# Forty modulation tiles moved from TensorE blocks in the first mixer to VectorE row products in three up projections

## The chip, the cores and the metric

One core of one Trainium2 chip runs the whole program. The metric is the device time of one execution in microseconds (us). The times are medians over runs of the same program. TensorE is called PE here, VectorE DVE, ScalarE ACT, GpSimd POOL and the engine that issues weight loads SP.

## The reference, cut to what matters

The reference is a stack of float32 layers on 256 tokens of width 1024, with 256 context tokens in its second half. First comes a block of an RWKV and a Hyena mixer, a convolutional feed-forward network, an embedding, attention, a second such network and embedding. Then follow two layers that are modulated by a condition:

```python
s_lat = jax.nn.silu(c)[:, None, :]
s_ctx = jax.nn.silu(c_ctx)
for l in range(DEPTH):                                   # DEPTH = 2
    ml = jnp.split(s_lat @ w_mod[l] + b_mod[l], 9, axis=-1)   # w_mod[l]: 1024 x 9216
    mc = jnp.split(s_ctx @ w_mod[l] + b_mod[l], 9, axis=-1)
    x = half_ffn(x, g_norm[l, 0], ml[0], ml[1], ml[2], ...)
    ...  # token mixing with ml[3:6], a second half_ffn with ml[6:9]
```

The two products with `w_mod` give 2 x 9216 numbers for each of the two conditions, that is 144 tiles of 128 numbers, kept in `sb_mod` as `mod[128, 144, 2]`. Each must be there before the layer that uses it: tiles 0 to 71 are layer 0 (its first half feed-forward uses 0 to 23), tiles 72 to 95 the first half feed-forward of layer 1, the rest what follows.

## The kernel before, in words

Activations lie with features on the 128 partitions. Weights stream through a ring of four buffers of 2 MB, loaded on SP's queue; a buffer is loaded again when the last matmul of its block is done.

The 144 tiles come from two mechanisms.

- **Row products on DVE.** A tile of 128 rows of the transposed `w_mod` (512 KB) is loaded on ACT's queue by `scalar_rows_load`, into one of three buffers in the convolutional feed-forward networks (44 tiles), and into one of two buffers in the half feed-forward networks. `vector_row(R, t, s)` multiplies it with the silu of condition s and sums along the row: one scalar_tensor_tensor of 128x1024, so two per tile. The load of tile t waits until both products of tile t - 2 are done.
- **Blocks on PE.** Ten blocks of four tiles (`MOD_BY_PE`) are computed in the RWKV and Hyena mixer. A block is a 2 MB load on SP, two pieces of eight matmuls of 32 output rows by 256 columns, a copy on ACT (L966), two narrow column matmuls that turn the row, and an addition on DVE (L975). `Fill` steps the four generators `tensor_modulation`, `scalar_modulation` and `vector_modulation` at fixed places: `to(n)` runs the generator up to step n. Pieces stand in `tensor_hyena`, after most steps of `tensor_lora`, ahead of the recurrence, one in each of the four scans, and a last pair of column matmuls behind them.

The order of each engine is written out by hand, and semaphores alone tie them together. In the mixer the path is: Hyena (transposes, 32 spectral matmuls, inverse), gate matmuls, eight low-rank steps n (two matmuls, then two Sigmoids on ACT, L623 and L624, double buffered), `scalar_prepare` and `vector_prepare` (the last instruction of the operands is L784), and the scans.

The three half feed-forward networks with 512 tokens (half00, half01, half10) each run `Fast`: an up projection of 22 iterations i = 0 to 21, each with seven products of Strassen's scheme in the order 1, 5, 6, 7, 3, 2, 4, then a down projection of four double iterations. In one iteration:

- PE's product 4 waits for `st_v` (L1706 on DVE), product 7 of the next iteration for `st_c21` (L1741), product 1 of the next for a Silu on ACT (L1636).
- DVE's order is: weight sum 0 of the next iteration (L1661), L1699, weight sums 1 and 2, L1706, L1708, L1710, L1713, weight sum 3, **middle rows**, L1741, two products into the hidden tile (L1750, L1753), **late rows**. Before, iterations 1 to 19 have one middle and one late row product. Iteration 20 has two middle ones, the addition of the bias (L1502), and then the first two weight sums of the down projection (128x1408) ahead of L1741.
- ACT loads row tile i in iteration i, right behind its copy of product 1 (L1629).
- SP's next 2 MB of weights are issued at the end of product 4 of odd iterations.

Of the kernel before, what the change touches and what calls it, by code (L numbers as in the profile page):

```python
# [40 lines left out]
ROWS_EACH, ROWS_CONV = 20, FT  # L41
MOD_BY_PE = [(0, 16), (0, 17)] + [(1, b) for b in (0, 1, 2, 3, 4, 5, 16, 17)]
# [57 lines left out]
def build(nc, ins, out):  # L100
# [346 lines left out]
    def tensor_idle(n):  # L447

        for _ in range(n):
            mm(aux[3][:, 0:128], ones[:], ones[:])  # L450
# [58 lines left out]
    def tensor_hyena(other):  # L509
        other.to(2)  # L510
# [6 lines left out]
        other.to(3)  # L517
# [10 lines left out]
        for ft in range(2):  # L528
            te.wait_ge(hy_prod.sem, hy_prod_at(ft))
            for ct in range(4):  # L530
                if ft == 0:
                    te.wait_ge(hy_spec.sem, hy_spec_at(4 + ct))
                for part in range(2):
                    ins_ = mm(aux[ct][:, 0:L], yri[:, part, ft, 128 * ct:128 * ct + 128], dft[:, 2 + part, ft, :],
                              ft + part == 0, ft + part == 2)
                if ft:
                    hy_inv.on(ins_)
            if ft == 0:
                other.to(4)
        other.to(5)  # L540

    def vector_hyena(other):
# [17 lines left out]
        other.to(4)  # L560
# [7 lines left out]
        other.to(5)  # L568

    def scalar_hyena(other):  # L570
        other.to(2)
        ac.wait_ge(hy_t.sem, hy_t_at(0))
        hy_tm.on(ac.copy(s_tm[:, 0, :], aux[0][:]))
        other.to(3)
# [7 lines left out]
        other.to(5)  # L582
# [31 lines left out]
    def scalar_lora(other, first):  # L614
# [5 lines left out]
        for n in range(NG):  # L620
# [4 lines left out]
            if 1 <= n < 7:  # L625
                other.to(5 + n)
# [3 lines left out]
    def tensor_lora(other, first):  # L630
# [8 lines left out]
        for n in range(NG):  # L639
# [7 lines left out]
            if 1 <= n < 7:  # L647
                other.to(5 + n)
# [13 lines left out]
    sil, pick = area(work, 12416, KT, 32), area(work, 12672, 2, 2)  # L662
# [16 lines left out]
    sil_set, pick_set = signal("condition_silu_set"), signal("partial_picker_set")  # L679
    sil_at, pick_at = sil_set.reserve(1), pick_set.reserve(1)  # L680
# [64 lines left out]
    def vector_prepare():  # L745
# [17 lines left out]
        yield  # L763
        shifted_mix(r_, 0)
        shifted_mix(v_, 16)
        yield
# [7 lines left out]
        yield  # L774
# [10 lines left out]
        yield  # L785
# [4 lines left out]
        yield  # L790
# [128 lines left out]

    mod_blocks = [(l, b, block(1, banks=(2, 3))) for l, b in MOD_BY_PE]  # L920
    n_mod = len(mod_blocks)
    mod_row, mod_cols = signal("modulation_row_copied"), signal("modulation_columns")
    mod_row_at, mod_cols_at = mod_row.reserve(n_mod), mod_cols.reserve(n_mod)
    mod_rows = (rs_buf, rope[:, 3, :])

    def sync_modulation():
        for l, b, blk in mod_blocks:
            wv = ins["w_mod_2"][l].rearrange("(k p) n -> p k n", p=128)
            sync_load(blk, [(slots[blk.slot][:, :].rearrange("p (k n) -> p k n", k=KT), wv[:, :, b * 512:b * 512 + 512])])

    def tensor_modulation():
        def columns(j):
            g, row = mod_blocks[j][2].groups[0], mod_rows[j % 2]
            te.wait_ge(mod_row.sem, mod_row_at(j))
            for c in range(2):
                ins_ = mm(acc[g.bank][:, 4 * c:4 * c + 4], row[:, 128 * c:128 * c + 128], area(work, 12672, 4))
            mod_cols.on(ins_)

        te.wait_ge(sil_set.sem, sil_at(0))
        te.wait_ge(pick_set.sem, pick_at(0))  # L940
        for j, (l, b, blk) in enumerate(mod_blocks):
            g = blk.groups[0]
            te.wait_ge(weights_in[blk.slot].sem, blk.arrived_at)
            if g.free_at:
                te.wait_ge(acc_free[g.bank].sem, g.free_at)
            w = slots[blk.slot][:, :].rearrange("p (k n) -> p k n", k=KT)
            for q in range(8):
                k, t = 2 * (q // 4) + q % 2, q % 4
                mm(acc[g.bank][32 * t:32 * t + 32, 0:256], sil[:, k, :], w[:, k, 256 * (t // 2):256 * (t // 2) + 256], q < 4, False)
            yield  # L950
            if j:
                columns(j - 1)
            for q in range(8):
                k, t = 4 + 2 * (q // 4) + q % 2, q % 4
                ins_ = mm(acc[g.bank][32 * t:32 * t + 32, 0:256], sil[:, k, :], w[:, k, 256 * (t // 2):256 * (t // 2) + 256], False, q >= 4)
            acc_full.on(ins_)
            yield
        columns(n_mod - 1)
        yield

    def scalar_modulation():
        for j, (l, b, blk) in enumerate(mod_blocks):
            g = blk.groups[0]
            yield
            ac.wait_ge(acc_full.sem, g.done_at)
            mod_row.on(ac.copy(mod_rows[j % 2][:, 0:256], acc[g.bank][:, 0:256]))  # L966
            yield
        yield

    def vector_modulation():  # L970
        def add(j):
            l, b, blk = mod_blocks[j]
            g, at = blk.groups[0], 72 * l + 4 * b
            ve.wait_ge(mod_cols.sem, mod_cols_at(j))
            acc_free[g.bank].on(ve.tensor_tensor(  # L975
                mod[:, at:at + 4, :].rearrange("p (n c) s -> p c n s", n=2), acc[g.bank][:, 0:8].rearrange("p (c n s) -> p c n s", c=2, n=2),
                cols("b_mod", 4, at).rearrange("p (n c) -> p c n", n=2).unsqueeze(3).to_broadcast([128, 2, 2, 2]), ALU.add))

        for j in range(n_mod):
            yield  # L980
            if j:
                add(j - 1)
            yield
        add(n_mod - 1)
        yield

    class Fill:


        def __init__(self, steps):  # L990
            self.steps, self.taken = steps, 0

        def to(self, count):
            while self.taken < count:
                self.taken += 1
                next(self.steps, None)

    MOD_STEPS, MOD_EARLY, MOD_FIRST = n_mod * 2 + 1, 11, 16  # L1000

    def scan_fill(p):
        return MOD_FIRST + (p + 1) * (MOD_STEPS - 1 - MOD_FIRST) // NP

# [27 lines left out]
    def tensor_scan(p, other, ahead):  # L1032
# [34 lines left out]
        other.to(scan_fill(p))  # L1067
# [102 lines left out]
    def scalar_scan(p, other, ahead):  # L1170
# [5 lines left out]
        for lv in range(1, 6):  # L1176
# [31 lines left out]
            if lv == 2:  # L1208
                a_step.on(ac.copy(dd, dd_next))
            elif lv == 3:  # L1210
                next(ahead, None)
                sc_kept.on(ac.copy(rho, kr[:, :, 1, :]))
            elif lv == 4:
                next(ahead, None)
            elif lv == 1:
                other.to(scan_fill(p))
# [6 lines left out]
    def vector_scan(p, other, ahead):  # L1223
# [11 lines left out]
        for lv in range(1, 6):  # L1235
# [22 lines left out]
            if lv == 1:  # L1258
                other.to(scan_fill(p))
# [27 lines left out]
    def tensor_recurrence(other, first):  # L1287
        for _ in first:
            pass
        other.to(MOD_FIRST)  # L1290
        for p in range(NP):
            tensor_scan(p, other, tensor_ahead(p + 1) if p + 1 < NP else iter(()))
        tensor_scan_out(NP - 1)
        other.to(MOD_STEPS)

    def scalar_recurrence(other, first):
# [3 lines left out]
        other.to(MOD_FIRST)  # L1300
        for p in range(NP):
            scalar_scan(p, other, scalar_ahead(p + 1) if p + 1 < NP else iter(()))
        scalar_scan_out(NP - 1)
        other.to(MOD_STEPS)

    def vector_recurrence(other):
        vector_scan_setup()
        for n, _ in enumerate(vector_prepare()):
            if n in (1, 2, 3):
                other.to((MOD_EARLY, MOD_FIRST - 2, MOD_FIRST)[n - 1])  # L1310
        for p in range(NP):
            vector_scan(p, other, vector_ahead(p + 1) if p + 1 < NP else iter(()))
        vector_scan_out(NP - 1)
        other.to(MOD_STEPS)

    def gpsimd_rope():
        gp.wait_ge(sc_out.sem, sc_out_at(NP - 1))
        g = mod_blocks[-1][2].groups[0]
        gp.wait_ge(acc_free[g.bank].sem, g.freed_at)
# [142 lines left out]
    class ModRows:  # L1462
        def __init__(self, first, n=ROWS_EACH, cond=row_cond, tiles=row_tile, junk=row_junk):
# [5 lines left out]
            self.done = rows_done.reserve(2 * n)  # L1469

# [149 lines left out]
    def scalar_fast(F, following=None):  # L1620
        u, v, g1, g2 = F.temps
        for i in range(F.start, F.n):
# [7 lines left out]
            if F.rows and 2 <= i < ROWS_EACH:  # L1630
                scalar_rows_load(F.rows, i)
# [41 lines left out]
    def vector_fast(F, gate_of=None, following=None):  # L1673
# [8 lines left out]
        for i in range(F.start, F.n):  # L1682
# [35 lines left out]
            if F.rows and 1 <= i <= ROWS_EACH:  # L1718
                vector_row(F.rows, i - 1, 0)
                if i == ROWS_EACH:  # L1720
                    vector_row(F.rows, i - 1, 1)
# [25 lines left out]
            else:  # L1747
# [6 lines left out]
                if F.rows and 1 <= i < ROWS_EACH:  # L1754
                    vector_row(F.rows, i - 1, 1)
# [836 lines left out]
    half00 = HalfFfn(0, 0, 0, ple1.x_ready, extra=(ctx_in, 32), squares=area(big, FT * L, KT, T2), rows=ModRows(2 * ROWS_CONV))  # L2592
    mix0 = Mixing(0, True, half00.x_ready, hooked=True)
    half01 = HalfFfn(0, 1, 0, mix0.x_ready, squares=area(big, 0, KT, T2), rows=ModRows(72 + 24))
    half10 = HalfFfn(1, 0, 0, half01.x_ready, squares=hook_sq, hooked=True, rows=ModRows(72 + 24 + ROWS_EACH))
# [3 lines left out]
    def sync_program():  # L2599
# [10 lines left out]
        sync_modulation()  # L2610
# [31 lines left out]
    def tensor_program():  # L2642
# [3 lines left out]
        fill = Fill(tensor_modulation())  # L2646
        tensor_hyena(fill)
        first = tensor_prepare()
        tensor_lora(fill, first)
        tensor_recurrence(fill, first)  # L2650
# [228 lines left out]
```

## Time and profile before

| | |
|---|---|
| Runs | 3010.04, 3012.65, 3015.83 us; median 3012.65 |
| Profiled execution | 3011.66 us |
| its span | 3010.4 us |
| PE busy | 2894.4 us, 96% |
| DVE busy | 1609.2 us, 53% |
| ACT busy | 614.1 us, 20% |
| mean granted PE clock | 0.993 of 2.4 GHz |

The span goes from the first to the last instruction; the execution is 1.3 us longer. The mixer with the PE blocks ends at 312 us. The three up projections lie at about 1070 to 1338, 1786 to 2050 and 2194 to 2461 us.

### The profile page before, as it was taken

The page shows a single profiled execution, that of the slowest core. Times are in us where ns is not written, and L with a number is a line of the kernel's source. Part 1 is how long each engine was busy: PE and PEld are TensorE (multiplying, and loading weights), DVE is VectorE, ACT ScalarE, POOL GpSimd, SP SyncE. Part 2 cuts the span into 40 slices and gives each one's busy share as a digit, 9 for nine tenths or more (in the row PEclk, how much of TensorE's full clock was granted, in tenths as well). Part 3 has the DMA queues.
Part 4 walks back from the last instruction along what each step waited for, and adds up shares of the span by engine and source line. Part 5 has one row for each costly group of instructions (what it writes and reads, how often), then busy time and mean ns, then how long its engine had stood idle before and what let it go on. Part 6 is the DMA issues. An engine that isn't in the chain of part 4 may idle for free.

```text
span 3010.4 us, 41500 instructions
## 1 busy us (share of the span) xinstructions
PE 2894.4 (96%) x17066; PEld 2364.9 (79%) x17066; DVE 1609.2 (53%) x3259; ACT 614.1 (20%) x1388; POOL 37.5 (1%) x60
## 2 busy tenths in 40 slices
PE   8988999998999999999998999999999999999999
PEld 7767788984888978888643458888878888765999
DVE  4367467435466466673314546665366663225675
ACT  1245221134221121000214520000020000224110
POOL 0000000020000000000000000000000000000000
PEclk9999999999999999999999999999999999999999
DMA  6551465662565633322303013432344323331444
GB/s 237 187 198 32 141 214 158 197 182 84 177 214 147 192 131 129 117 79 77 112 26 112 29 56 126 137 117 58 110 146 131 120 72 81 110 108 55 142 142 111
DMA packets 344496, 376.17 MB, mean 125 GB/s; under 512 B 8723, under 2 KB 283556, under 8 KB 343540
## 3 DMA queue, kind: packets, MB, share of 16 engines
q1 hardware_dynamic: 324788, 306.65, 32.8%
q10 hardware_dynamic: 17312, 61.55, 5.6%
q0 software_dynamic: 2208, 5.31, 0.9%
q8 instruction: 137, 2.24, 0.3%
q14 instruction: 51, 0.42, 0.0%
HBM read 372.44 MB, written 1.05 MB: 124 GB/s over the span
## 4 chain that ended last, share of the span: by engine, by line
PE 90%; DVE 5%; ACT 4%; issue 1%; DMA 0%; ACTq 0%; DVEq 0%
PE acc L135 75%; PE aux L135 14%; ACT sb_xn L283 1%; PE aux L2433 1%; ACT L272 0%; DVE sb_work L2159 0%; DVE sb_work L2156 0%; ACT sb_work L1958 0%; ACT sb_work L1960 0%; DVE sb_xn L259 0%; DVE sb_work L1661 0%; PE acc L1045 0%; ACT sb_rstd L274 0%; DVE sb_work L1938 0%; DVE sb_work L2170 0%
## 5 line engine op out<-in xcount | busy, mean ns | idle before, releaser
L135 PE MATMUL acc<-sb_xn,weights 128*128 128x256 f32 (+2 forms) x5184 | 1217.7, 390 | 22.3 <-DVE sb_xn L259 14.0
L135 PEld LDWEIGHTS acc<-sb_xn,weights 128*128 128x128 f32 x5184 | 946.7, 191 | 247.5 <-issue 125.2
L135 PE MATMUL acc<-sb_work 128*128 128x256 f32 (+1 forms) x1944 | 375.0, 346 | 0.0
L135 PEld LDWEIGHTS acc<-sb_work 128*128 128x128 f32 x1944 | 324.4, 191 | 34.7 <-issue 0.4
L135 PE MATMUL acc<-sb_work,weights 128*128 128x256 f32 (+2 forms) x1508 | 322.4, 361 | 3.2 <-DVE sb_work L1394 1.4
L135 PE MATMUL acc<-sb_big,weights 128*128 128x256 f32 (+1 forms) x1776 | 313.8, 333 | 3.9 <-DVE sb_work L1815 3.8
L135 PEld LDWEIGHTS acc<-sb_big,weights 128*128 128x128 f32 x1776 | 278.1, 191 | 30.6 <-issue 5.2
L135 PEld LDWEIGHTS acc<-sb_work,weights 128*128 128x128 f32 x1508 | 254.2, 191 | 50.5 <-issue 21.8
L1629 ACT COPY sb_work<-acc 128x256 f32<-128x256 f32 (+1 forms) x112 | 38.0, 339 | 690.2 <-PE acc L135 690.2
L1699 DVE TENSOR_TENSOR sb_work<-sb_work,acc 128x256 f32<-128x256 f32 (+1 forms) x112 | 42.6, 381 | 228.8 <-PE acc L135 228.8
L135 PE MATMUL aux<-sb_xn,sb_work 128*128 128x256 f32 (+1 forms) x704 | 152.2, 360 | 8.4 <-ACT sb_xn L283 8.4
L1634 ACT ACTIVATE sb_work<-sb_work 128x256 f32<-128x256 f32 (+1 forms) x88 | 34.4, 391 | 572.4 <-DVE sb_work L1713 572.4
L1661 DVE TENSOR_TENSOR sb_work<-weights 128x512 f32<-128x512 f32 (+1 forms) x112 | 99.7, 890 | 95.5 <-PE acc L135 95.1
L135 PEld LDWEIGHTS aux<-sb_xn,sb_work 128*128 128x128 f32 x704 | 123.7, 194 | 24.3 <-issue 10.0
L135 PE MATMUL aux<-sb_big,sb_work 128*128 128x128 f32 (+3 forms) x592 | 109.3, 339 | 0.0
L1741 DVE TENSOR_TENSOR sb_work<-sb_work,acc 128x256 f32<-128x256 f32 (+1 forms) x112 | 42.5, 379 | 116.0 <-PE acc L135 115.9
L1661 DVE TENSOR_TENSOR weights<-weights 128x512 f32<-128x512 f32 (+1 forms) x112 | 99.6, 890 | 3.0
L1661 DVE TENSOR_TENSOR sb_work<-sb_work,weights 128x512 f32<-128x512 f32 (+1 forms) x112 | 99.2, 886 | 2.8 <-issue 0.2
L1661 DVE TENSOR_TENSOR sb_work<-weights,sb_work 128x512 f32<-128x512 f32 (+1 forms) x112 | 99.1, 884 | 0.7
L1713 DVE TENSOR_TENSOR sb_work<-sb_work,aux 128x256 f32<-128x256 f32 (+1 forms) x112 | 42.4, 378 | 104.2 <-PE aux L135 104.2
L135 PEld LDWEIGHTS aux<-sb_big,sb_work 128*128 128x128 f32 (+1 forms) x592 | 88.7, 185 | 10.9 <-issue 2.8
L135 PE MATMUL acc<-sb_xn,sb_work 128*128 128x128 f32 (+1 forms) x528 | 91.8, 331 | 4.2 <-DVE sb_xn L1666 4.2
(353 smaller groups left out, 2716.0 us busy)
## 6 DMA issues: line engine op xcount, KB each, us to landing
weights<-ffn_w_up SPq DMA_DIRECT2D x88, 1024.0 KB, 9.1
weights<-ffn_w_down SPq DMA_DIRECT2D x48, 1408.0 KB, 7.2
weights<-ffn_w_gate SPq DMA_DIRECT2D x44, 1024.0 KB, 5.4
sb_work<-w_mod_rows ACTq DMA_DIRECT2D x60, 512.0 KB, 6.2
sb_big<-w_mod_rows ACTq DMA_DIRECT2D x44, 512.0 KB, 4.8
weights<-w_mod SPq DMA_DIRECT2D x10, 2048.0 KB, 8.1
weights<-w_in SPq DMA_DIRECT2D x8, 2048.0 KB, 8.7
weights<-mix_w_in SPq DMA_DIRECT2D x6, 2048.0 KB, 12.5
```

Of the source, the lines that this page charges most:

```text
L135: return te.matmul(o, lhsT, rhs, start=start, stop=stop, skip_group_check=True)
L283: shifted.on(ac.activation(y, y, ACT.Identity, bias=N.shift(k, h)))
L1629: st_u.on(ac.copy(u[:, s, :], bank_a[:, 0:F.H]))
L1634: st_g2.on(ac.activation(g2[:, s, :], g2[:, s, :], ACT.Silu))
L1661: st_s.on(ve.tensor_tensor(to, one, other, op))
L1699: st_b.on(ve.tensor_tensor(u, u, bank_b[:, 0:F.H], ALU.add))
L1713: st_c12.on(ve.tensor_tensor(g2, g2, bank_e[:, 0:F.H], ALU.add))
L1741: st_c21.on(ve.tensor_tensor(u, u, bank_c[:, 0:F.H], ALU.add))
L2433: ins_ = te.transpose(aux[u % 3][:, c:c + 128], mx_e[:, u % 4, W * i + 128 * kt:W * i + 128 * kt + 128], ident[:])
```

## The change

```diff
-ROWS_EACH, ROWS_CONV = 20, FT
-MOD_BY_PE = [(0, 16), (0, 17)] + [(1, b) for b in (0, 1, 2, 3, 4, 5, 16, 17)]
+ROWS_HALF, ROWS_UNTIL, ROWS_CONV = (34, 33, 33), 20, FT
...
+            self.upto = lambda i: 2 * n * i // ROWS_UNTIL
...
-            if F.rows and 2 <= i < ROWS_EACH:
-                scalar_rows_load(F.rows, i)
+            if F.rows and 2 <= i <= ROWS_UNTIL:
+                for t in range(F.rows.upto(i - 2) // 2 + 2, min(F.rows.upto(i - 1) // 2 + 2, F.rows.n)):
+                    scalar_rows_load(F.rows, t)
...
-            if F.rows and 1 <= i <= ROWS_EACH:
-                vector_row(F.rows, i - 1, 0)
-                if i == ROWS_EACH:
-                    vector_row(F.rows, i - 1, 1)
+            if F.rows and 1 <= i <= ROWS_UNTIL:
+                middle = (F.rows.upto(i - 1) + F.rows.upto(i) + 1) // 2 if i < ROWS_UNTIL else F.rows.upto(i)
+                for n in range(F.rows.upto(i - 1), middle):
+                    vector_row(F.rows, n // 2, n % 2)
+                if i == ROWS_UNTIL:
                     vector_rows_bias(F.rows)
...
-                if F.rows and 1 <= i < ROWS_EACH:
-                    vector_row(F.rows, i - 1, 1)
+                if F.rows and 1 <= i < ROWS_UNTIL:
+                    for n in range(middle, F.rows.upto(i)):
+                        vector_row(F.rows, n // 2, n % 2)
```

Beside this, `sync_modulation`, `tensor_modulation`, `scalar_modulation`, `vector_modulation`, `Fill` and every `other.to(...)` are deleted, with the first Silu of the condition on ACT (L2670) and two small instructions on DVE (L2695, L2697) that served the blocks. half00 takes tiles 44 to 77, half01 78 to 110, half10 111 to 143. The number of row buffers (two) and their size stay.

## Rows read from the trace of the kernel before

**Rows 1.** The page's chain that ended last, shares of the span by engine.
```profile
PE 90%; DVE 5%; ACT 4%; issue 1%; DMA 0%; ACTq 0%; DVEq 0%
```

**Rows 2.** Timeline from 118 us: start, duration, engine, line, operation, count [idle before].
```profile
124.03 1.07 PE L135 MATMUL acc<-weights,sb_work 128*32 128x256 f32 x16
...
142.75 1.07 PE L135 MATMUL acc<-weights,sb_work 128*32 128x256 f32 x16
...
151.08 0.47 ACT L623 ACTIVATE sb_work<-aux,sb_cols 128x256 f32<-128x256 f32 x1
...
157.94 1.67 PE L135 MATMUL acc<-weights,sb_work 128*32 128x256 f32 x16 [4.30 <-DVE sb_mod L975]
```

**Rows 3.** Timeline from 160 us, the end of the preparation of the first scan.
```profile
172.31 1.28 ACT L1297 ACT_TABLE_LOAD   x1
...
175.83 0.63 ACT L805 ACTIVATE sb_work<-sb_work 128x512 f32<-128x512 f32 x1
...
177.50 0.68 DVE L776 TENSOR_TENSOR sb_work<-sb_work 128x512 f32<-128x512 f32 x1
...
180.75 0.69 DVE L784 TENSOR_TENSOR sb_work<-sb_work 128x512 f32<-128x512 f32 x1
```

**Rows 4.** Busy time of PE, PEld, DVE, ACT, POOL by stretch; PEclk, DMA share, GB/s.
```profile
159.00:165.00 6.00, 6.00 (x40) 2.74 (x36) 0.17 (x1) 2.19 (x5) 0.00 (x0) 0.50 0.25 77
...
171.00:177.00 6.00, 3.97 (x44) 2.08 (x43) 0.97 (x3) 5.20 (x9) 0.00 (x0) 1.00 1.04 375
```

**Rows 5.** Timeline from 211 us, the second scan, and from 308 us.
```profile
217.99 0.65 DVE L1231 TENSOR_TENSOR sb_xn<-sb_big 128x512 f32<-128x512 f32 x1
...
218.75 1.15 PE L135 MATMUL aux<-sb_big,sb_xn 64*64 64x64 f32 x32 [0.17 <-issue]
...
312.48 0.61 PE L135 MATMUL acc<-sb_work,sb_rope 128*128 128x4 f32 x4
```

**Rows 6.** Timeline of ACT from 0 and from 570 us: the first Sin, a table load.
```profile
24.97 0.42 ACT L440 ACTIVATE sb_work<-sb_work 64x256 f32<-64x256 f32 x1 [10.66 <-DVE sb_work L415]
...
588.23 1.28 ACT L1869 ACT_TABLE_LOAD   x1
592.61 0.38 ACT L1869 ACTIVATE sb_work<-acc 128x256 f32<-128x256 f32 x1 [3.09 <-PE acc L135]
```

**Rows 7.** Timeline from 1150 us, one iteration of half00's up projection (an odd one).
```profile
1159.19 0.34 ACTq L1476 DMA_DIRECT2D sb_work<-w_mod_rows  x1
...
1160.44 0.69 DVE L1661 TENSOR_TENSOR sb_work<-weights 128x512 f32<-128x512 f32 x1 [1.29 <-PE acc L135]
...
1163.90 0.42 DVE L1706 TENSOR_TENSOR sb_work<-sb_work,acc 128x256 f32<-128x256 f32 x1
...
1167.08 1.89 PE L135 MATMUL acc<-sb_work,weights 128*128 128x256 f32 x8
...
1171.27 0.33 ACTq L1476 DMA_DIRECT2D sb_work<-w_mod_rows  x1
```

**Rows 8.** Row loads: KB each, us to landing, in windows 1159:1161, 2294:2296, 1267:1269.
```profile
sb_work<-w_mod_rows ACTq DMA_DIRECT2D x1, 512.0 KB, 3.5
...
sb_work<-w_mod_rows ACTq DMA_DIRECT2D x1, 512.0 KB, 6.4
...
sb_work<-w_mod_rows ACTq DMA_DIRECT2D x1, 512.0 KB, 7.4
```

**Rows 9.** A wait of PE in the timeline, and the stretch behind it as in rows 4.
```profile
718.17 1.12 PE L2082 MATMUL aux<-sb_ident,sb_work 128*128 128x128 f32 x4 [3.18 <-DVE sb_work L2170]
...
718.00:720.00 2.00, 1.83 (x8) 1.42 (x10) 1.90 (x7) 0.79 (x4) 0.00 (x0) 0.51 1.10 360
```

**Rows 10.** Timeline from 1300 us, iterations 20 and 21 of half00's up projection.
```profile
1324.95 1.23 DVE L1496 SCALAR_TENSOR_TENSOR sb_work<-sb_work 128x1024 f32<-128x1024 f32 x1
...
1329.85 0.41 DVE L1741 TENSOR_TENSOR sb_work<-sb_work,acc 128x256 f32<-128x256 f32 x1
...
1331.11 1.89 PE L135 MATMUL acc<-sb_xn,weights 128*128 128x256 f32 x8
```

More of the change, by code:

```diff
@@ L445, in scalar_filter, with tensor_idle @@
             filt_rn.on(ac.activation(f_rn, f_rn, ACT.Exp, scale=-0.5))
-    def tensor_idle(n):
+    def tensor_idle(n, bank=aux[3]):
         for _ in range(n):
-            mm(aux[3][:, 0:128], ones[:], ones[:])
+            mm(bank[:, 0:128], ones[:], ones[:])
     def tensor_mix_in():
@@ L506, in build, with tensor_hyena @@
     hy_bias_at = hy_bias.reserve(4)
-    def tensor_hyena(other):
-        other.to(2)
+    def tensor_hyena():
         te.wait_ge(filt_ready.sem, filt_ready_at(3))
@@ L516, in tensor_hyena @@
         hy_t.on(ins_)
-        other.to(3)
         te.wait_ge(ctx_in.sem, 32)
@@ L537, in tensor_hyena, with vector_hyena @@
                     hy_inv.on(ins_)
[L538 to L542, printed above, removed]
+    def vector_hyena():
         ve.wait_ge(hy_t.sem, hy_t_at(0))
@@ L567, in vector_hyena, with scalar_hyena @@
             hy_out.on(ve.tensor_tensor(yb[:, ct, :], s_fm[:, ct, :], uhy[:, ct, :], ALU.mult))
-        other.to(5)
-    def scalar_hyena(other):
-        other.to(2)
+    def scalar_hyena():
         ac.wait_ge(hy_t.sem, hy_t_at(0))
         hy_tm.on(ac.copy(s_tm[:, 0, :], aux[0][:]))
-        other.to(3)
         for n in range(8):
@@ L612, in scalar_gate_input, with scalar_lora @@
         gd_moved.on(ac.copy(gd2, gd))
-    def scalar_lora(other, first):
+    def scalar_lora(first):
         ac.wait_ge(wad_set.sem, wad_set_at(1))
@@ L624, in scalar_lora, with tensor_lora @@
             lora_read.on(ac.activation(aa[:, g, :], aux[2 * (n % 2) + 1][:, 0:L], ACT.Sigmoid, bias=cols("a0", 1, g)))
-            if 1 <= n < 7:
-                other.to(5 + n)
             if n == 3:
                 next(first)
-    def tensor_lora(other, first):
+    def tensor_lora(first):
         te.wait_ge(up_in.sem, 48)
@@ L918, in tensor_ahead @@
         yield
[L920 to L1003, printed above, removed]
     def tensor_scan_out(p):
@@ L1030, in build, with tensor_scan @@
     BY_IDENT = (3, 4)
-    def tensor_scan(p, other, ahead):
+    def tensor_scan(p, ahead):
         def times(out_bank, lhs, rhs_, start=None):
@@ L1066, in tensor_scan @@
         turned(kr[:, :, 0, :], b1)
-        other.to(scan_fill(p))
         for lv in range(1, 6):
@@ L1168, in tensor_scan, with scalar_scan @@
                 sc_y.on(local_out((b0, b1), 1))
-    def scalar_scan(p, other, ahead):
+    def scalar_scan(p, ahead):
         for hp in range(2):
@@ L1221, in scalar_scan, with vector_scan @@
         sc_tc.on(ac.copy(tc[:, 1], b0[:, 0:128].rearrange("p (g t) -> p g t", g=2)))
-    def vector_scan(p, other, ahead):
+    def vector_scan(p, ahead):
         for hp in range(2):
@@ L1285, in vector_scan, with tensor_recurrence, scalar_recurrence @@
                                  quads((b0, b1)[par][:, 256:512]).rearrange("p (g a) t -> p g a t", g=2), ALU.add))
-    def tensor_recurrence(other, first):
+    def tensor_recurrence(first):
         for _ in first:
             pass
-        other.to(MOD_FIRST)
         for p in range(NP):
-            tensor_scan(p, other, tensor_ahead(p + 1) if p + 1 < NP else iter(()))
+            tensor_scan(p, tensor_ahead(p + 1) if p + 1 < NP else iter(()))
         tensor_scan_out(NP - 1)
-        other.to(MOD_STEPS)
-    def scalar_recurrence(other, first):
+    def scalar_recurrence(first):
         ac.preload_act_table_set(NAT_LOG)
@@ L1299, in scalar_recurrence, with vector_recurrence @@
             pass
-        other.to(MOD_FIRST)
         for p in range(NP):
-            scalar_scan(p, other, scalar_ahead(p + 1) if p + 1 < NP else iter(()))
+            scalar_scan(p, scalar_ahead(p + 1) if p + 1 < NP else iter(()))
         scalar_scan_out(NP - 1)
-        other.to(MOD_STEPS)
-    def vector_recurrence(other):
+    def vector_recurrence():
         vector_scan_setup()
-        for n, _ in enumerate(vector_prepare()):
-            if n in (1, 2, 3):
-                other.to((MOD_EARLY, MOD_FIRST - 2, MOD_FIRST)[n - 1])
+        vector_prepare()
         for p in range(NP):
-            vector_scan(p, other, vector_ahead(p + 1) if p + 1 < NP else iter(()))
+            vector_scan(p, vector_ahead(p + 1) if p + 1 < NP else iter(()))
         vector_scan_out(NP - 1)
-        other.to(MOD_STEPS)
     def gpsimd_rope():
         gp.wait_ge(sc_out.sem, sc_out_at(NP - 1))
-        g = mod_blocks[-1][2].groups[0]
-        gp.wait_ge(acc_free[g.bank].sem, g.freed_at)
         rope_in.on(gp.dma_start(rope[:, :, 0:L], ins["c_rope"]))
@@ L1462, in build, with __init__ @@
     class ModRows:
-        def __init__(self, first, n=ROWS_EACH, cond=row_cond, tiles=row_tile, junk=row_junk):
+        def __init__(self, first, n, cond=row_cond, tiles=row_tile, junk=row_junk):
             self.first, self.n, self.silu_cond, self.tiles, self.junk = first, n, cond, tiles, junk
@@ L2591, in build @@
     ple1 = Ple(1, ffn1.x_ready)
-    half00 = HalfFfn(0, 0, 0, ple1.x_ready, extra=(ctx_in, 32), squares=area(big, FT * L, KT, T2), rows=ModRows(2 * ROWS_CONV))
+    half00 = HalfFfn(0, 0, 0, ple1.x_ready, extra=(ctx_in, 32), squares=area(big, FT * L, KT, T2), rows=ModRows(2 * ROWS_CONV, ROWS_HALF[0]))
     mix0 = Mixing(0, True, half00.x_ready, hooked=True)
-    half01 = HalfFfn(0, 1, 0, mix0.x_ready, squares=area(big, 0, KT, T2), rows=ModRows(72 + 24))
-    half10 = HalfFfn(1, 0, 0, half01.x_ready, squares=hook_sq, hooked=True, rows=ModRows(72 + 24 + ROWS_EACH))
+    half01 = HalfFfn(0, 1, 0, mix0.x_ready, squares=area(big, 0, KT, T2), rows=ModRows(2 * ROWS_CONV + ROWS_HALF[0], ROWS_HALF[1]))
+    half10 = HalfFfn(1, 0, 0, half01.x_ready, squares=hook_sq, hooked=True, rows=ModRows(2 * ROWS_CONV + sum(ROWS_HALF[0:2]), ROWS_HALF[2]))
     mix1 = Mixing(1, False, half10.x_ready, hooked=True)
@@ L2645, in tensor_program @@
         tensor_mix_in()
-        fill = Fill(tensor_modulation())
-        tensor_hyena(fill)
+        tensor_hyena()
         first = tensor_prepare()
-        tensor_lora(fill, first)
-        tensor_recurrence(fill, first)
+        tensor_lora(first)
+        tensor_recurrence(first)
         tensor_mix_out()
@@ L2669, in scalar_program @@
         ac.wait_ge(const_in.sem, 64)
-        sil_set.on(ac.activation(sil[:, :, 0:2], cols("cond", 16).rearrange("p (k s) -> p k s", s=2), ACT.Silu))
         scalar_mix_in()
         scalar_gate_input()
-        fill = Fill(scalar_modulation())
-        scalar_hyena(fill)
+        scalar_hyena()
         first = scalar_prepare()
-        scalar_lora(fill, first)
-        scalar_recurrence(fill, first)
+        scalar_lora(first)
+        scalar_recurrence(first)
         scalar_group_norm()
@@ L2694, in vector_program @@
         vector_norm(mix_norm, constants=True)
-        v_step.on(ve.memset(sil[:, :, 2:32], 0.0))
         v_step.on(ve.tensor_reduce(quarters[:], ident[:].rearrange("p (j s) -> p s j", s=32), AX.X, ALU.add))
-        pick_set.on(ve.tensor_reduce(pick, ident[:].rearrange("p (n j s) -> p n s j", n=2, s=32)[:, :, 0:2, :], AX.X, ALU.add))
         vector_mix_in()
-        fill = Fill(vector_modulation())
-        vector_hyena(fill)
-        vector_recurrence(fill)
+        vector_hyena()
+        vector_recurrence()
         vector_group_norm()
```

17 lines of the change are left out of this document (removed).

## The prediction

> **What bounds the kernel now.** I read the chain of waits first: nine tenths of the path are PE [rows 1]. So work on PE costs its full length wherever nothing else is late, and work on DVE or ACT costs only where PE waits for it. Then I read the timeline of the stretch that loses the PE blocks, and the timeline of one iteration that gains row products. These are two different places: the first (121 to 182 us) is a latency chain over three engines, the second is PE at work without a pause, with DVE beside it.
>
> **Removed: the blocks in Hyena and the low-rank steps.** One piece of eight matmuls takes 1.0 us of PE [rows 2]. I rebuilt the schedule without the pieces, step by step.
>
> The first three pieces stand around the transposes, which need the last Hyena product of DVE anyway; 0.5 us is saved there. The spectral matmuls bound PE after that. The column pass and piece at 142.4 to 143.8 (the piece is at 142.75) go whole, 1.3, and so does the piece after the inverse, 1.0 of the same form. So the Sigmoid that starts at 151.08 starts at 148.2 [rows 2].
>
> From there ACT sets the pace: 16 Sigmoids at 0.37 from start to start are 5.9 us, two activations of `scalar_prepare` between them 1.4, and waits for the short low-rank matmuls 0.8. The last Sigmoid ends at 156.3, where before it ended at 172.3, just ahead of the table load [rows 3]. The pieces had stretched these steps: PE stood 4.3 us behind a piece's DVE addition, which is queued behind five mixing instructions [rows 2], and then worked at 1.2 GHz from 158.4 to 165.1 [rows 4].
>
> From the table load at 172.31 to the end of L805 (175.83 + 0.63) there are 4.15 us, which stay: 160.45. L776 started at 177.50 only because DVE first had to serve a block's addition; now it follows at 160.5. L784 ends 3.94 us after L776 starts [rows 3]: 164.4 where it was 181.44. **Gross gain 17.0 us.** DVE is no obstacle: its own chain (scan, three mixes, four instructions behind the key norm) ends at 157.6.
>
> Against it stands the clock. PE now has nothing between the bonus matmul (158.7) and 164.4. A pause of 4.3 us was followed by 1.2 GHz for 6.7 us [rows 2, 4]; 66% busy at 171 to 177 us was not [rows 4]. So the scan starts at 1.2 GHz. Its first PE step (1.1 us on the path) doubles, then five us belong to ACT and DVE, then one or two us run at half speed: 2.2 us lost. Bounds: 0 if the clock stays, and 5.5 if the low-rank steps run slow as well (2.1) and the slow stretch is as long as 6.7 us of pure matmul (3.4).
>
> The four pieces inside the scans give nothing: the next matmuls start 0.1 us after L1231 on DVE ends [rows 5], and that chain has no piece in it. The last column pass (312.48) stands ahead of the output projection; 0.4 goes [rows 5]. ACT's copies and DVE's additions go with the blocks; beyond the above they sat in idle time. The 20 MB of block loads on SP are off the path; their going brings the next loads forward, for which nobody waited. The added row loads are as many bytes.
> Sum: -17.0 - 0.4 + 2.2 = **-15.2 us**.
>
> **Removed: the first Silu.** Its table served the Sin at 24.97, on the path. The next load must then stand ahead of that Sin. Where an activation waits, the trace has its load ahead of the wait (load 588.23, activation 592.61) [rows 6]: 0. If it stood behind the wait it would be 1.28, the duration of that load.
> The Trainium skill (ScalarE: Activation LUTs, What happens when an exp ACTIVATE runs) says that the compiler puts the load right before the activation, and that a switch costs about 2.7 us with its drain. By that, 2.7 would come on top of the sum; the 4.4 us between the two starts at 588 us speak against it.
>
> **Added: 80 row products on DVE.** One takes 1.23 us, 1.26 with the read of its sum [rows 10]. Instead of two, iterations 1 to 19 have three or four. An iteration lasts 12.08 us (1159.19 to 1171.27) [rows 7]. DVE has weight sums of 4 x 0.69, seven small ones at about 0.38, and two rows, in all 7.9 us; with four rows 10.5. That fits. The middle rows push L1741, which has 5 us to spare; the late rows end as the next weight sum may start. Compute time alone costs PE nothing.
>
> **Added: a wait for the tile.** Let u(i) = 2n*i//20 be the row products done after iteration i. ACT loads tile t in the first iteration i with u(i-1) >= 2t-2. DVE may need its first product in iteration d as soon as u(d) >= 2t+1. Where u goes from an odd number by four, d is one iteration before the load. For n = 34 that is 13 to 17, 23 to 27, 47 to 51 and 57 to 61 (d = 5, 8, 15, 18); for n = 33 9 to 13, 19 to 23 and 29 to 33 (d = 4, 7, 10). Ten times DVE stands at its last late row of iteration d until ACT has copied product 1 of d+1, issued the load, and it has landed. Queued behind it are weight sum 0, L1699, sums 1 and 2 and L1706, for which product 4 of d+1 waits.
>
> Take zero at 1158.65, the end of product 1 in d. The issue is at 0.54 + 12.08 = 12.6 [rows 7]. After a landing time T come the row (1.26), three weight sums (2.05) and L1699 and L1706 (0.8): L1706 ends at 16.7 + T. Product 4 of d+1 is due at 8.43 + 12.08 = 20.5 [rows 7]. The delay is T - 3.8. Loads issued in odd iterations land in 3.5 us, in even ones in 6.1 to 8.2, beside SP's 2 MB [rows 8]. So the six with even d cost nothing. The four with odd d (5, 15, 7, 7) load at the places where the trace has 6.5, 7.4, 6.6 and 6.4, of which the ends stand in the trace rows [rows 8]: 2.7 + 3.6 + 2.8 + 2.6 = **11.7 us**. Bounds: 0 (DVE's chain shorter by its overlaps, T of 3.5) and 18 (8.2 each).
>
> Each of these is a pause of PE of about 3 us. One of 3.18 us left the clock at 1.2 GHz for 3.3 us [rows 9], a loss of 1.7. Shorter ones do so only at times: I take three of four, **5.1 us** (0 to 6.8).
>
> **Iteration 20.** Four rows stand ahead of the two large weight sums and L1741, where there were two: +2.5. L1741 then ends at 1332.8, but product 7 of iteration 21 started at 1331.11 [rows 10]. PE waits 1.7; in three networks **5.1 us** (3 to 7; a late tile 33 would add up to 1 each).
>
> **Sum.** -15.2 + 11.7 + 5.1 + 5.1 = +6.7. The profiled execution took 3011.66 us, its span 3010.4: 3018.4. The median of the runs shown is 1.0 above that execution: **3019.4 us**.
>
> **The rivals.**
> - *The tiles come in time enough* (ends on the other side). Place: product 4 of d+1. If the late row starts less than 3.8 us after its load's issue also in even iterations, or the chain behind it is some 3 us shorter, PE does not wait. It decides at T = 3.8. Only iteration 20 costs: -15.2 + 5.1 = -10, 3002.5 us. For it: 3.5 us in every odd iteration. Against: every even one is at 6.1 or more.
> - *A colder mixer.* PE at 1.2 GHz already in the low-rank steps and long into the scan: a gain of 11.9 in place of 15.2 (or less, if a scan at 80% of PE keeps the low clock longer), 3022.7 to 3025. For it: 1.2 GHz lasted 6.7 us under full work [rows 4]. Against: 66% busy held 2.4 GHz [rows 4].
> - *Two tiles in one queue.* ACT now issues two loads together, beside 2 MB of weights. If landings go to 9 to 10 us in even iterations, the four waits cost 23 and the middle rows of other even iterations wait too, past the one us that DVE has to spare: +18 or so, 3030 us. For it: the two loads at a network's start took 10.9 and 12.0. Against: there they followed the condition's 1 MB and several MB of weights.
>
> **How the numbers follow.** A measurement of this kernel can tell about 0.2%, 6 us, from no change. Forecast 0.55, with an own range of 3012 to 3026; tiles in time 0.17; colder mixer 0.13; two tiles 0.13; the rest 0.02. Slower by over 0.2% (above 3018.7): 0.6 of the forecast, nearly all of the two slow cases: 0.56. Within: 0.26. Faster (below 3006.6): 0.18, the third case and a thin edge of the forecast. The range that holds 8 in 10 is 3005 to 3031.
>
> **What would show it.** L784 ends near 164.4 (right for the first part), with PEclk 0.5 behind it and no matmul that waits on a piece. In each up projection, L1496 idles before a late row in iterations 5, 8, 15, 18 or 4, 7, 10 with the DMA as its releaser, 3.5 us after the issue in even d and over 6 in odd; behind an odd one PE waits some 3 us on L1706 for its product 4, with PEclk at 0.5 for about 3 us. In iteration 21 PE waits 1.7 on L1741. The prediction is wrong if those idle times of DVE are missing, if PE stays busy through the three up projections, or if the first scan starts after 168.

## The result and the profile after

The changed kernel takes 3022.72 us (median of 20 runs, 3012.93 to 3027.69) and the kernel before 3014.78 (20 runs, 3007.70 to 3020.41): a ratio of 1.0025, 95% interval 1.0018 to 1.0033. It is slower by 7.9 us by the medians (5.4 to 9.9 by the interval), where +6.7 was forecast.

The two profiled executions stand further apart: 3025.75 and 3011.66 us, 14.1. So the traces can't be subtracted without care; how much of it lies in places that the change doesn't touch is worked out below.

The chain's shares in the page of the changed kernel, beside [rows 1]:

```profile
PE 87%; DVE 6%; ACT 4%; issue 2%; DMA 1%; ACTq 0%; DVEq 0%
```

DMA has come onto the chain. It is the row products (L1375, which was L1496) that wait for it. The view of that line has DVE's idle time before them:

```profile
its engine sat idle before it (us, times) until:
  DMA sb_work<-w_mod_rows: 45.5, 12
```

In the kernel before, DVE never waited there. The timeline of PE shows whom that reaches: matmuls that wait for L1586 (was L1706) are product 4 of an iteration, those that wait for L1622 (was L1741) stand in iteration 21.

```profile
1148.06 3.19 PE L134 MATMUL acc<-sb_work,weights 128*128 128x256 f32 x8 [2.54 <-DVE sb_work L1586]
1273.00 1.99 PE L134 MATMUL acc<-sb_work,weights 128*128 128x256 f32 x8 [2.12 <-DVE sb_work L1586]
1329.78 1.97 PE L134 MATMUL acc<-sb_xn,weights 128*128 128x256 f32 x8 [1.26 <-DVE sb_work L1622]
...
1895.83 3.44 PE L134 MATMUL acc<-sb_work,weights 128*128 128x256 f32 x8 [2.41 <-DVE sb_work L1586]
...
2050.99 1.97 PE L134 MATMUL acc<-sb_xn,weights 128*128 128x256 f32 x8 [1.25 <-DVE sb_work L1622]
...
2313.39 1.99 PE L134 MATMUL acc<-sb_work,weights 128*128 128x256 f32 x8 [2.35 <-DVE sb_work L1586]
...
2466.87 1.97 PE L134 MATMUL acc<-sb_xn,weights 128*128 128x256 f32 x8 [1.26 <-DVE sb_work L1622]
```

Seven waits, four and three, two of the four in half00 and one in each other half: the forecast's places. Together 13.2 us. Behind two of the four the eight matmuls last 3.19 and 3.44 us in place of 1.89 [rows 7]: most of them ran at half the clock.

One of the four from the inside. ACT issues tiles at 1136.93 and, right behind it, the next; DVE stands at its late row until 1144.17, 7.2 us after the issue. Queued behind it is the chain to L1586 (timeline of ACT's queue and of DVE, changed kernel):

```profile
1136.93 0.87 ACTq L1355 DMA_DIRECT2D sb_work<-w_mod_rows  x2
```

```profile
1144.17 1.23 DVE L1375 SCALAR_TENSOR_TENSOR sb_big<-sb_work 128x1024 f32<-128x1024 f32 x1 [6.74 <-DMA sb_work<-w_mod_rows]
...
1145.33 0.69 DVE L1541 TENSOR_TENSOR sb_work<-weights 128x512 f32<-128x512 f32 x1
...
1147.59 0.42 DVE L1586 TENSOR_TENSOR sb_work<-sb_work,acc 128x256 f32<-128x256 f32 x1
...
1181.17 1.23 DVE L1375 SCALAR_TENSOR_TENSOR sb_big<-sb_work 128x1024 f32<-128x1024 f32 x1 [2.99 <-DMA sb_work<-w_mod_rows]
```

The last of these lines is the other kind: three iterations later DVE waits 2.99 us for its load, and PE doesn't notice. Four of DVE's twelve waits last 6.3 to 6.7 us, six last 3.0 to 3.1, two 0.2 and 0.6.

Now the early part. The end of the first mixer block and the preparation of the first scan, in the timeline of the changed kernel, beside [rows 3, 6]:

```profile
24.61 1.28 ACT L439 ACT_TABLE_LOAD   x1 [11.69 <-DVE sb_work L414]
25.90 0.42 ACT L439 ACTIVATE sb_work<-sb_work 64x256 f32<-64x256 f32 x1
...
26.37 1.11 PE L134 MATMUL aux<-sb_work 64*64 64x256 f32 x2 [2.71 <-ACT sb_work L439]
27.41 6.24 PE L134 MATMUL acc<-sb_xn,weights 128*128 128x256 f32 x16
...
125.94 0.44 PE L513 MATMUL aux<-sb_ident,sb_big 128*128 128x128 f32 x2 [1.50 <-DVE sb_big L481]
127.25 22.72 PE L134 MATMUL aux<-sb_work 128*128 128x512 f32 x64 [0.88 <-DVE sb_work L538]
...
167.76 0.69 DVE L763 TENSOR_TENSOR sb_work<-sb_work 128x512 f32<-128x512 f32 x1
168.50 2.89 PE L134 MATMUL aux<-sb_work 64*64 64x128 f32 x32 [5.33 <-DVE sb_work L763]
```

The table load stands behind the Sin's wait, on the path. L763 (was L784) ends at 168.45, 13.0 us earlier than before [rows 3], and not at 164.4. The clock behind it, by stretches (columns as in [rows 4]):

```profile
160.00:164.00 4.00, 1.52 (x2) 0.30 (x2) 1.52 (x3) 3.94 (x7) 0.00 (x0) 0.78 0.00 0
164.00:168.00 4.00, 0.00 (x0) 0.00 (x0) 3.43 (x6) 0.47 (x1) 0.00 (x0) 0.50 0.00 0
168.00:172.00 4.00, 3.50 (x35) 3.17 (x36) 1.90 (x4) 1.14 (x2) 0.00 (x0) 0.50 0.00 0
```

I follow the pair by four matmuls that both kernels have. First the kernel before, then the changed one (timeline of PE):

```profile
331.90 8.47 PE L135 MATMUL acc<-sb_work,weights 128*128 128x256 f32 x38 [1.39 <-DVE sb_work L1394]
...
1070.29 3.75 PE L135 MATMUL aux<-sb_xn,sb_work 128*128 128x256 f32 x8 [2.00 <-ACT sb_xn L283]
...
1782.94 3.65 PE L135 MATMUL aux<-sb_xn,sb_work 128*128 128x256 f32 x8 [2.58 <-ACT sb_xn L283]
...
2194.69 2.46 PE L135 MATMUL aux<-sb_xn,sb_work 128*128 128x256 f32 x8 [2.59 <-ACT sb_xn L283]
```

```profile
320.12 14.08 PE L134 MATMUL acc<-sb_work,weights 128*128 128x256 f32 x64 [1.39 <-DVE sb_work L1272]
...
1060.68 3.75 PE L134 MATMUL aux<-sb_xn,sb_work 128*128 128x256 f32 x8 [2.00 <-ACT sb_xn L282]
...
1785.73 2.52 PE L134 MATMUL aux<-sb_xn,sb_work 128*128 128x256 f32 x8 [2.59 <-ACT sb_xn L282]
...
2203.36 3.65 PE L134 MATMUL aux<-sb_xn,sb_work 128*128 128x256 f32 x8 [2.59 <-ACT sb_xn L282]
```

The differences are -11.8 at the output projection, -9.6 at half00, +2.8 at half01, +8.7 at half10, +14.0 at the end. So the stretches from the start of one network to the start of the next (the last to the end) cost 12.4, 5.9 and 5.3 us, 23.6 in all, against the 9.6 that was left of the early gain of 11.8. PE's idle time in the three stretches rose by 5.7, 3.7 and 3.5 (12.9: the seven waits). The time lost to the clock (one minus the granted clock, summed over stretches of 4 us) rose by 6.8, 1.7 and 1.8. Of these 10.3 us, 3.4 stand right behind two of the seven waits. Nearly all of the rest is in three drops, near 1648, 1714 and 2812 us, in code that the change doesn't touch. One of them is in the token mixing behind half00, where the kernel before has none near it:

```profile
1713.00:1717.00 4.00, 3.33 (x10) 0.99 (x10) 0.00 (x0) 0.59 (x1) 0.00 (x0) 0.50 0.00 0
```

By the starts of the same matmuls, half00's up projection cost 8.3 of the 12.4 us (a group of 22 in its down projection starts at 1341.51, and at 1342.77 in the kernel before), and the other 4.1 came behind it, where the drops near 1648 and 1714 stand.

The mean granted clock differs between executions of one kernel too: in the 20 runs of the changed kernel it goes from 0.991 in the run of 3012.93 us to 0.985 in that of 3027.69. The traced execution (0.986) is one of its slower ones, while the trace of the kernel before (0.993) is one of the faster of its kind. That is why the pair stands 14.1 us apart and the medians 7.9.

### The profile page after: what moved, and what is told of

It reads as the page before. It is cut to its first block, busy times and chain, and to the rows that moved or that the text cites. A ratio compares the mean times of both kernels' runs of the same rounds, so it can differ in the third digit from the quotient of the medians.

```text
span 3024.4 us, 40936 instructions
## 1 busy us (share of the span) xinstructions
PE 2887.1 (95%) x16706; PEld 2361.9 (78%) x16706; DVE 1698.4 (56%) x3407; ACT 610.0 (20%) x1377; POOL 37.4 (1%) x60
## 4 chain that ended last, share of the span: by engine, by line
PE 87%; DVE 6%; ACT 4%; issue 2%; DMA 1%; ACTq 0%; DVEq 0%
PE acc L134 73%; PE aux L134 13%; ACT sb_xn L282 1%; DMA sb_work<-w_mod_rows 1%; PE aux L2315 1%; DVE sb_work L1541 1%; ACT L271 0%; DVE sb_work L2041 0%; DVE sb_work L2038 0%; ACT sb_work L1840 0%; DVE sb_big L1375 0%; DMA weights<-mix_w_in 0%; ACT sb_work L1842 0%; DVE sb_work L1375 0%; DVE sb_work L2052 0%
## 5 line engine op out<-in xcount | busy, mean ns | idle before, releaser
L1579 DVE TENSOR_TENSOR sb_work<-sb_work,acc 128x256 f32<-128x256 f32 (+1 forms) x112 | 42.6, 380 | 218.4 <-PE acc L134 218.4
L1375 DVE SCALAR_TENSOR_TENSOR sb_big<-sb_work 128x1024 f32<-128x1024 f32 x100 | 122.1, 1221 | 45.5 <-DMA sb_work<-w_mod_rows 45.5
L1375 DVE SCALAR_TENSOR_TENSOR sb_work<-sb_work 128x1024 f32<-128x1024 f32 x100 | 122.2, 1222 | 1.4
L134 PE MATMUL aux<-sb_work 64*64 64x128 f32 (+8 forms) x526 | 82.8, 377 | 15.7 <-DVE sb_work L763 5.3
## 6 DMA issues: line engine op xcount, KB each, us to landing
weights<-mix_w_in SPq DMA_DIRECT2D x6, 2048.0 KB, 11.8
```

The costliest lines, as they stand in the source:

```text
L134: return te.matmul(o, lhsT, rhs, start=start, stop=stop, skip_group_check=True)
L1375: rows_done.on(ve.scalar_tensor_tensor(row if s else R.junk, row, 1.0, R.silu_cond[:, s, :], ALU.mult, ALU.mult, accum_out=mod[:, R.first ...
L1579: st_b.on(ve.tensor_tensor(u, u, bank_b[:, 0:F.H], ALU.add))
```

## The experiments

Each was timed beside the kernel before, five times or more. A ratio is to that kernel, with its 95% interval; 1 thousandth is 3.0 us. The changed kernel's own ratio is 1.0025.

**One tile in each iteration (e_rows20).**

```diff
-ROWS_HALF, ROWS_UNTIL, ROWS_CONV = (34, 33, 33), 20, FT
+ROWS_HALF, ROWS_UNTIL, ROWS_CONV = (20, 20, 20), 20, FT
...
+        v_step.on(ve.memset(mod[:].rearrange("p a b -> p (a b)"), 0.0))
```

> The changed kernel with 20 row products in each half-row up projection in place of 34, 33 and 33: one tile in every iteration, as before the change. The 40 tiles that are then left out stay zero, so part of the modulation is not computed. Only the early part of the change (blocks gone, Silu gone) is left in the time. By my prediction's sum it would be 15.2 us faster than the kernel before (ratio 0.995). By the theory formed on the changed kernel's trace (the table load of 1.28 us stands ahead of the Sin on the path, and the first layer behind it runs at half clock) it is 11 to 12 us faster, ratio 0.996, and no up projection has a wait of PE over 1 us for DVE. The rival, that the cost sits in the early part or in the tail and not in the up projections, would give no gain here.

2998.93 us, ratio 0.9951 (0.9936 to 0.9965): 14.8 us faster (10.5 to 19.3). The seven waits are gone; only the early part is left. The predicted -15.2 and the -11 to -12 of the theory from the trace both lie in the interval, the first nearer to its middle. No gain at all is refuted. This kernel leaves 40 tiles out, so it shows a price and is no version to use.

**The new rows on top of the old blocks (e_both).**

It is the kernel before with its blocks and its Silu, and with the new rows: the lines below, cut, and the new middle and late rows as shown in the section on the change.

```diff
-ROWS_EACH, ROWS_CONV = 20, FT
+ROWS_HALF, ROWS_UNTIL, ROWS_CONV = (34, 33, 33), 20, FT
...
+            self.upto = lambda i: 2 * n * i // ROWS_UNTIL
...
-            if F.rows and 2 <= i < ROWS_EACH:
-                scalar_rows_load(F.rows, i)
+            if F.rows and 2 <= i <= ROWS_UNTIL:
+                for t in range(F.rows.upto(i - 2) // 2 + 2, min(F.rows.upto(i - 1) // 2 + 2, F.rows.n)):
+                    scalar_rows_load(F.rows, t)
...
```

> The kernel before with its modulation blocks on PE and its first Silu kept, and only the new schedule of 34, 33 and 33 row products added (40 tiles are computed twice, nothing is left out). It holds the cost alone. Theory: 4 waits of PE at product 4 (2.1 to 2.5 idle each), the half-rate stretch behind them, and 3 waits of 1.26 in iteration 21: the difference of the traces at the up projections' starts says 12.4 + 5.9 + 5.3 = 23.6 at most, my prediction's terms 21.9, the idle rows alone 13.2. So +13 to +24, likeliest +18 (ratio 1.006), with the same seven waits of PE in its trace. Rival: the waits come only because the early part shifted the loads, then there are none here and the time is that of before.

3038.88 us, ratio 1.0073 (1.0056 to 1.0091): 22.0 us slower (16.9 to 27.4), where the sum's terms gave 21.9. PE's timeline has the same seven waits, at 2.17, 3.41, 2.26 and 2.29 us for product 4 and 1.25 to 1.26 in iteration 21. So they don't depend on the early part. The two parts add up: -14.8 + 22.0 = +7.2, with +7.5 (1.0025) for the whole.

The runs' clocks say what the 22 us are made of. The mean granted clock is 0.9914 in the 18 runs of the kernel before beside this one and 0.9887 here; it is 0.9896 with 20 rows each and 0.9870 in the 20 runs of the changed kernel. Both steps are what the new rows add, and both are about 0.0027, or 8 us of time lost to the clock (8.6 and 8.1 from the single runs, each give or take 3). The rest of the mean times rises by 14.8 and 13.4 us, which is the size of the seven waits (13.2). So the rows do lower the clock on average, though no run shows at which places, beyond those right behind the waits.

**The Silu back (e_silu).**

```diff
+        a_step.on(ac.activation(small[:, 44:60], cols("cond", 16), ACT.Silu))
```

> The changed kernel with one Silu of the condition put back on ACT ahead of the wait for the first block, so that the table is loaded early and the Sin finds it. Nothing of the result changes. Theory: the load's 1.28 us go from the path, the pause of PE before the second matmul of the first block falls from 2.71 to about 1.3, its clock stays at 2.4 GHz and the Hyena stage starts 2.5 to 3 us earlier: 3 us faster than the changed kernel, ratio to before about 1.0015 in place of 1.0025. Rival: the load was hidden in the changed kernel too, and the later start came from elsewhere (a late weight load, a later condition): no change in the trace at the end of the first block.

3021.32 us, ratio 1.0017 (1.0006 to 1.0028). That is 2.4 us below the changed kernel's ratio, but the intervals overlap, so the time alone decides nothing. The timeline does:

```profile
24.90 0.42 ACT L439 ACTIVATE sb_work<-sb_work 64x256 f32<-64x256 f32 x1 [10.63 <-DVE sb_work L414]
...
25.37 0.64 PE L134 MATMUL aux<-sb_work 64*64 64x256 f32 x2 [1.35 <-ACT sb_work L439]
25.94 3.72 PE L134 MATMUL acc<-sb_xn,weights 128*128 128x256 f32 x16
...
163.42 0.69 DVE L763 TENSOR_TENSOR sb_work<-sb_work 128x512 f32<-128x512 f32 x1
164.16 2.89 PE L134 MATMUL aux<-sb_work 64*64 64x128 f32 x32 [5.57 <-DVE sb_work L763]
```

No load ahead of the Sin, the pause 1.35 in place of 2.71, and the sixteen matmuls behind it 3.72 us in place of 6.24. In this execution L763 ends at 164.11: 17.3 us before the 181.44 of [rows 3], where 17.0 was worked out. The load's own price is 1.35 us, shown in every execution without the Silu (the pause is 2.70 or 2.71 in all four of them). The further 3 us between this trace and the changed kernel's are clock: the drop ahead of 32 us (3.0, of which 1.3 fall into a wait for the next Sin that PE has here anyway) and one in the spectral matmuls (22.72 us against 21.03), less 0.4 for an earlier start. That second drop also came in two kernels with the Silu, so it isn't the load's. The first stands right behind the longer pause in three of the four traces without the Silu and in none of the six with it, so it may well belong to the load; four traces don't prove it.

**Row products in whole tiles (e_even).**

```diff
-            self.upto = lambda i: 2 * n * i // ROWS_UNTIL
+            self.upto = lambda i: 2 * (n * i // ROWS_UNTIL)
```

> The changed kernel with row products given out in whole tiles: an iteration has two or four of them, and none starts a tile in the iteration before the one that loads the next but one. All tiles are computed. Theory: the four waits of PE for product 4 go (9.4 us of idle time and the half-rate matmuls behind two to four of them), the three in iteration 21 stay, so 12 to 15 us faster than the changed kernel: ratio to before about 0.998. Rival: DVE's added work is what delays PE (iterations with four rows are here as many or more): then as many waits of the same length stand at other iterations and the ratio stays 1.0025.

3005.42 us, ratio 0.9973 (0.9960 to 0.9986): 15.7 us less than the changed kernel, and faster than the kernel before. All four waits for product 4 are gone, and DVE's idle time on the line falls from 45.5 us in twelve waits to this:

```profile
  DMA sb_work<-w_mod_rows: 0.4, 1
```

The three waits in iteration 21 stay (1.29, 1.26, 1.26). DVE does the same work, with four row products in more iterations (14 of half00's 20, against 8). So the rival (DVE's load delays PE) falls: it was the slip of one product across an iteration's border. Of the 15.7 us, 9.4 are the idle time of the four waits; the rest isn't placed.

**One tile in iteration 20 as well (e_even_last).**

```diff
-            self.upto = lambda i: 2 * (n * i // ROWS_UNTIL)
+            self.upto = lambda i: 2 * (n if i >= ROWS_UNTIL else (n - 1) * i // (ROWS_UNTIL - 1))
```

> The changed kernel with row products in whole tiles and the whole tiles spread so that iteration 20 has one (two row products) in place of two. All tiles are computed. Whole tiles alone gave a ratio of 0.9973 to the kernel before. Theory: the three waits of 1.26 us in iteration 21 (L1622) go as well, and whatever half-rate stretch stood behind them: 3.8 to 5.1 us less, ratio about 0.996. Rival: these waits only take the place of another one right behind (the gate's product or the next load), then the time stays that of whole tiles, 0.9973.

3002.03 us, ratio 0.9955 (0.9943 to 0.9968), 5.4 us below whole tiles (intervals overlap). Iterations 20 and 21 of half00 in PE's timeline, without a wait:

```profile
1322.77 1.89 PE L134 MATMUL aux<-sb_xn,sb_work 128*128 128x256 f32 x8
1324.50 1.89 PE L134 MATMUL acc<-sb_xn,weights 128*128 128x256 f32 x8
```

The waits' removal is shown by the trace, their price of 3.8 us by the idle times; the time agrees within its width. With all 100 tiles it stands level with the kernel of 60 (0.9955 and 0.9951): the extra 80 products cost nothing that can be measured once their order is right.

**The same with the Silu (e_last_silu).** Both edits above.

> Whole tiles with one tile in iteration 20, and the Silu of the condition back ahead of the first block's wait. Nothing is left out. Theory: it has the early part with its table load hidden (the Silu alone gave 0.8 thousandths, its trace 2.7 us at the entry of the Hyena stage) and none of the seven waits: about 3013 - 14.4 (the early part, as 20 row products showed) - 2.5 = 2996, ratio 0.994 to 0.995. Rival: the clock takes back what the table load gave, then it equals whole tiles with one in iteration 20 alone (about 0.996).

3000.67 us, ratio 0.9949 (0.9935 to 0.9962). The load's 1.35 is too small to be told from 0.9955.

**Matmuls in the pause ahead of the scan (e_warm).** The Silu is back here too.

```diff
-    scan_banks = [acc_free[b].planned for b in range(2)]
+    scan_banks = [acc_free[b].planned for b in range(3)]
...
+        te.wait_ge(acc_free[2].sem, scan_banks[2])
+        tensor_idle(8, acc[2])
...
+        tensor_idle(20, acc[2])
```

> The changed kernel with the Silu put back and 28 idle matmuls on PE: 8 behind the low-rank steps and 20 behind the bonus matmul, in the pause ahead of the scan. Theory: the pause of about 5.5 us ahead of the scan's first matmul has left the clock at 1.2 GHz (granted 0.50 from 164 to 172 us in the changed kernel); with matmuls in it the first 32 matmuls of the scan last 1.1 to 1.4 us in place of 2.89, and the scan ends about 2 us earlier: ratio about 1.001 where the Silu alone gave 1.0017. Rival: the matmuls stand in the way of the short low-rank ones or of the scan's own, or the clock falls anyway (in a bf16-free stretch so short that it isn't held): no gain or 1 us lost.

3019.80 us, ratio 1.0016 (1.0007 to 1.0025): the same as the Silu alone. The first matmuls are fast (1.59 us for 32 in place of 2.89), but in this execution the clock falls a little later. These are the stretches of this kernel:

```profile
164.00:168.00 4.00, 2.38 (x40) 1.97 (x36) 3.07 (x7) 1.09 (x2) 0.00 (x0) 1.00 0.02 4
168.00:172.00 4.00, 3.40 (x74) 3.43 (x76) 1.85 (x4) 2.22 (x6) 0.00 (x0) 0.77 0.00 0
```

From the end of the operands to the output projection it takes 151.0 us; 151.6 in the Silu's kernel, 151.7 in the changed one, 150.5 in the kernel before. So in this pair the cold clock costs the scan 1.2 us, and the idle matmuls give back half of it. One trace each is thin, though: the six kernels that enter the scan cold take from 150.6 to 153.1 (mean 151.7), the two with blocks 150.2 and 150.5. In the trace of everything together, the other kernel with idle matmuls, the clock stays at 1.00 from 160 to 180 us, and the stretch takes 149.6. The 2 us that I expected don't show in the time, whose intervals are too wide to exclude them.

**Everything together (e_all).** Whole tiles, one in iteration 20, the Silu, the idle matmuls.

> Everything together: whole tiles, one in iteration 20, the Silu back, the idle matmuls ahead of the scan. Nothing is left out. Theory: 2 us less than the same without the idle matmuls, near 2994 us or a ratio of 0.993 to 0.994. Rival: the idle matmuls give nothing, and the two have one ratio.

2997.94 us, ratio 0.9938 (0.9925 to 0.9950). It beats both kernels: 18.7 us (15 to 23) under the one before. Its distance from the version without idle matmuls (0.9949), 3.3 us, is within the intervals, so what the idle matmuls give stays open.

## Why the prediction was right

Its steps, one by one:

- *Early part, -15.2.* Measured alone: -14.8. Inside it two terms were wrong in opposite directions. **The table load was priced at 0 and costs 1.35** (its duration of 1.28, the bound that the text had named, and the pause that it lengthens). This is the step that failed: "where an activation waits, the trace has its load ahead of the wait" was a rule made from one row [rows 6]. The kernel before had the other kind too, at its first load, and I hadn't looked for it. The cold scan was priced at 2.2 and costs 1.2 in the traced pair (about 1.4 over the six cold traces, which spread over 2.4). The gross 17.0 is 17.3 in the trace with the load hidden. By my own list the prediction would be "wrong if the first scan starts after 168": it started at 168.50, for the load and two drops of the clock, not because a step of the chain was missing.
- *Four waits for the tile, 11.7.* They stand where u(i) put them, 9.4 us in all. The rule T - 3.8 gives 3.4 for the first one's 7.2, and the wait was 2.54: product 4 came due 8.6 us after the issue and not 7.9, and the chain behind the landing took 3.8 and not 4.1. The six of even iterations cost nothing, as said.
- *The clock behind them, 5.1.* Two of four had a drop of about 1.7 us in the trace: 3.4. Over all runs the clock lost about 8 us to the new rows, so this term was too small: it counted only the places right behind the four waits.
- *Iteration 20, 5.1.* 3.8 idle (1.26, 1.25 and 1.26, against 1.7 each).
- *The whole cost of the rows, 21.9.* Measured alone: 22.0 (16.9 to 27.4). That the sums agree so closely is partly luck: 16.8 of idle time were forecast and 13.2 stand in the trace, 5.1 of clock were forecast and about 8 are in the runs. Two errors of some 3 us cancel. The mechanism is right in each of its places; the sizes are not.

The rivals: *tiles in time enough* falls with the 6.3 to 6.7 us waits of DVE. *A colder mixer* falls by the trace: in the changed kernel the granted clock is 1.00 through the low-rank steps, from 152 to 160 us. The time of the early part alone (14.8, interval 10.5 to 19.3) would not exclude its 11.9. *Two tiles in one queue* falls: the first of two loads issued together landed in 7.2 us and not in 9 to 10, and no wait of PE grew to the 6 us each that 23 in all would take. The landings do vary: over the sixteen such waits in four traces they come 6.6 to 8.5 us after the issue, and the longest waits of PE (3.41, 3.57 and 3.75 us) stand behind the three that take over 8.

The Trainium skill (ScalarE: Activation LUTs, What happens when an exp ACTIVATE runs) says that the compiler puts the load right before the activation. In the order of ACT's instructions the trace agrees: nothing stands between the two. In time they can be apart: at this Sin they follow each other (24.61, then 25.90), while the load at 578.09 ran 4.4 us ahead of an activation that had to wait. The page's 2.7 us with the drain isn't seen: the load lasted 1.28 and moved PE by 1.35. Even between two activations without a wait, at 172.31 in the kernel before, the next one starts 1.30 us after the load does.

## What to carry to other kernels

- When a stream of double-buffered tiles is spread over iterations by a fraction, list for each iteration the first product against the load's issue. A product that slips over the border waits for a whole transfer with everything queued behind it. Rounding the spread to whole tiles made the same work 15.7 us cheaper.
- An activation that is dropped may have been the one that loaded the table early. Price the load at its full duration at the next user unless every row of that kind says otherwise.
- Before two traces are subtracted, take the clock's drops out of both, and look at the granted clock of every run. Here some 6 of the 14 us between them were drops at places that the change doesn't touch.

## What was not expected of the hardware

- Whether a pause lets the clock drop isn't decided by its length alone. Of sixteen waits for product 4 in the traces of four kernels, nine had half the clock behind them (2.17, 2.26, 2.28, 2.41, 2.49, 2.54, 3.41, 3.57, 3.75 us) and seven did not (1.92, 2.08, 2.12, 2.25, 2.29, 2.35, 2.38): between 2.17 and 2.38 both occur.
- The first big matmuls of the program (16 from about 16 us) last 3.69 us in five of the profiled executions (one of each kernel) and 5.25 to 5.38 in the other five, with the same work ahead of them. The Trainium skill (TensorE: Matmul & The Clock Gate, Part 1: The HAM clock gate) says that how many matmuls run slow at a kernel's start differs between runs of one kernel; these ten executions fit that.
- A table load may stand on either side of its activation's wait: in the changed kernel it ran early at 79.31 and 578.09, and behind the wait at 6.48 and 24.61. What decides it is open.
